# Attention's output product: eight fp32 blocks become split blocks with three fp32r products each

## What is computed

```python
def stick_breaking_attention(q, k, v):
    ...
        z = jnp.einsum('bhqd,bhkd->bhqk', q[:, :, q0:end], k[:, :, :end]).astype(jnp.float32) * scale
        ...
        log_stay = jnp.where(mask, -jax.nn.softplus(z), 0.0)
        stay_after = lax.cumsum(log_stay, axis=3, reverse=True) - log_stay
        log_w = jax.nn.log_sigmoid(z) + stay_after
        w = jnp.where(mask, jnp.exp(log_w), 0.0)
        o = jnp.einsum('bhqk,bhkd->bhqd', w, v[:, :, :end].astype(jnp.float32))

def stick_breaking_block(h, k, v, w_q, q_gain, w_o):
    q = rms_norm_2(heads(h @ w_q), q_gain)
    o = stick_breaking_attention(q, k, v)
    o = o.transpose(0, 2, 1, 3).reshape(Bt, S, D_ATTN)
    return o @ w_o

        x = x + stick_breaking_block(h, k_shared, v_shared, b_w_q[j], q_norm[j], b_w_o[j])
        x = x + 0.5 * swiglu(rms_norm_2(x, ffn2_norm[l]), ffn2_w13[l], ffn2_w2[l])
```

## Time and profile before

| | us |
|---|---|
| median of three executions | 1619.96 |
| the profiled execution | 1619.76 |
| its span, first to last instruction | 1618.0 |
| TensorE busy | 1571.3 (97%) |
| GpSimd busy | 917.8 (57%) |
| VectorE busy | 1035.1 (64%) |
| ScalarE busy | 737.9 (46%) |

### The profile page before, as it was taken

The page is one execution under the profiler, slowest core; times in us unless marked ns, Lnnn a source line. Parts: engine busy times, 40 slices in busy tenths (PEclk is TensorE's granted clock), DMA queues, the critical chain, the costliest instruction groups (busy, mean ns, idle before and its releaser), DMA issues.

```text
span 1618.0 us, 24581 instructions
## 1 busy us (share of the span) xinstructions
PE 1571.3 (97%) x9562; PEld 1361.0 (84%) x9562; DVE 1035.1 (64%) x1432; ACT 737.9 (46%) x1071; POOL 917.8 (57%) x1090
## 2 busy tenths in 40 slices
PE   7999999999999998999999999999999999899998
PEld 6888888877788887888888788888888888778887
DVE  6866565654686668966356686656676655468663
ACT  5554432022555454555333554555555553355452
POOL 6866520200796676966201796676977671179664
PEclk9999999999999999999999999999999999999999
DMA  7655532221465563655354465564465561146553
GB/s 269 208 185 184 180 118 93 79 73 51 164 208 183 182 202 122 211 193 168 134 180 145 157 215 181 177 221 144 151 216 185 171 215 40 66 157 214 185 173 117
DMA packets 107203, 263.65 MB, mean 163 GB/s; under 512 B 9168, under 2 KB 43088, under 8 KB 106960
## 3 DMA queue, kind: packets, MB, share of 16 engines
q1 hardware_dynamic: 107088, 262.09, 47.6%
HBM read 261.00 MB, written 1.05 MB: 162 GB/s over the span
## 4 chain that ended last, share of the span: by engine, by line
PE 90%; DVE 6%; ACT 1%; DMA 1%; issue 1%; POOL 1%; SPq 0%; DVEq 0%; ACTq 0%
PE ps L1597 39%; PE ps L1598 22%; PE ps L1645 9%; PE ps L1691 5%; PE ps L1600 4%; PE ps L1769 1%; DMA raw<-blocks 1%; DVE xn L903 1%; PE ps L1867 1%; DVE arena L1547 1%; PE ps L2066 1%; PE ps L1629 1%; PE ps L1630 1%; PE ps L1631 1%; PE ps L1661 1%
## 5 line engine op out<-in xcount | busy, mean ns | idle before, releaser
L517 POOL TENSOR_TENSOR w_lo<-raw,w_hi 128x256 fp32r<-128x256 f32 x1056 | 899.1, 885 | 582.9 <-ACT w_hi L595 579.3
L1597 PE MATMUL ps<-xn,w_hi 128*128 128x512 f32 x1848 | 664.4, 398 | 18.7 <-DVE xn L903 6.9
L1598 PE MATMUL ps<-xn,w_lo 128*128 128x256 f32 x2112 | 552.4, 281 | 0.0
L595 ACT ACTIVATE w_hi<-raw 128x1024 fp32r<-128x1024 f32 (+1 forms) x492 | 451.3, 927 | 211.3 <-PE ps L1600 114.4
L1597 PEld LDWEIGHTS ps<-xn,w_hi 128*128 128x128 f32 x1848 | 348.4, 189 | 98.2 <-DVE xn L903 10.0
L1598 PEld LDWEIGHTS ps<-xn,w_lo 128*128 128x128 f32 x2112 | 400.8, 190 | 17.3
L1597 PE MATMUL ps<-hid,w_hi 128*128 128x512 f32 x1008 | 363.6, 397 | 0.5 <-DVE w_lo L895 0.5
L1598 PE MATMUL ps<-hid,w_lo 128*128 128x256 f32 x1056 | 292.6, 282 | 0.0
L895 DVE TENSOR_TENSOR w_lo<-raw,w_hi 128x512 fp32r<-128x512 f32 (+1 forms) x222 | 253.0, 1140 | 33.1 <-ACT w_hi L595 28.1
L1597 PEld LDWEIGHTS ps<-hid,w_hi 128*128 128x128 f32 x1008 | 190.2, 189 | 41.9 <-issue 0.8
L982 DVE TENSOR_TENSOR arena<-ps,low_part 128x512 f32<-128x512 f32 x132 | 90.8, 688 | 200.4 <-ACT low_part L656 200.4
(11 more groups left out here) (320 smaller groups left out, 1243.6 us busy)
## 6 DMA issues: line engine op xcount, KB each, us to landing
raw<-blocks SPq DMA_DIRECT2D x419, 512.0 KB, 3.5
raw<-blocks SPq DMA_DIRECT2D x144, 256.0 KB, 3.5
cst<-consts SPq DMA_DIRECT2D x1, 2358.0 KB, 15.2
x<-x_in SPq DMA_DIRECT2D x4, 256.0 KB, 6.8
out<-x SPq DMA_DIRECT2D x4, 256.0 KB, 3.3
cst<-consts SPq DMA_DIRECT2D x1, 109.0 KB, 2.0
```

What stands on the lines that cost most here:

```text
L517: ins = nc.gpsimd.tensor_tensor(w_lo[:, slot(n), piece], raw[:, slot(n), piece], w_hi[:, slot(n), piece], ALU.subtract)
L595: nc.scalar.activation(w_hi[:, slot(n), cols], raw[:, slot(n), cols], ACT.Copy)\
L1597: nc.tensor.matmul(where, hi, both.rearrange("p a t -> p (a t)"), start=opens, stop=False)
L1598: ins = nc.tensor.matmul(where[:, 0:SEQ], lo, high, start=False, stop=False)
```

## The change

The eight blocks of w_o become split blocks (`split_out`), and the attention's outputs are split too: ScalarE writes the high half of pair c into `xn[:, c, 0, :]`, and VectorE subtracts it from the PSUM bank into `xn[:, c, 1, :]` (`y_low`). TensorE runs `output_rows` in place of `add_direct`: 24 fp32r matmuls for each block. Low parts of blocks 3, 5 and 7 are made on VectorE behind its loop, those of 0, 1, 2, 4 and 6 on GpSimd; before block 4 GpSimd waits until VectorE's eight products are done. ScalarE converts blocks 0 to 2 ahead of its first sigmoid. Ahead of the norm it now converts up to the third block of `ffn_f`, and the fourth and fifth stand inside the norm. Other phases' lists are unchanged.

```diff
-    add("attn_out", ["rows"] * 8)
+    add("attn_out", ["split_out"] * 8)
...
+def attn_out_on_vector(i):
+
+    return i in (3, 5, 7)
...
+                if phase == "attn_out":
+                    for i in range(KD):
+                        if i == 3:
+                            need(pool, "at_w", KD)
+                        if not attn_out_on_vector(i):
+                            lo(n0 + i)
...
+                    if a < len(late):
+                        hi_until(late[a])
                     nc.scalar.activation(squares(a, gains), pair_of_x(a), ACT.Square).then_inc(sq_ready, 1)
...
                 preload(ACT.Sigmoid)
+                hi_until(out_rows + 2)
                 need(act, "at_sep", 1)
...
                 def output(c):
                     need(act, "at_o", c + 1)
-                    nc.scalar.activation(y[:, c, :], bank(6 + c % 2)[:, 0, :], ACT.Copy).then_inc(ev["at_y"], 1)
+                    nc.scalar.activation(xn[:, c, 0, :], bank(6 + c % 2)[:, 0, :], ACT.Copy).then_inc(ev["y_hi"], 1)
...
-                hi_until(FIRST["attn_out"] + 8 + 4)
+                hi_until(out_rows + 8 + 2)
...
-                lambda: (norm(9, "g_ffn_f"), ffn(5, FIRST["ffn_f"]), hi_until(end)),
+                lambda: (norm(9, "g_ffn_f", late=(0, FIRST["ffn_f"] + 3, FIRST["ffn_f"] + 4)), ffn(5, FIRST["ffn_f"]), hi_until(end)),
...
+                def y_low(c):
+                    need(v, "y_hi", Y_BEFORE["attn_out"] + c + 1)
+                    signal(tt(xn[:, c, 1, :], bank(6 + c % 2)[:, 0, :], xn[:, c, 0, :], ALU.subtract), "y_lo")
...
                     if c == 1:
                         scaled_queries(3)
+                    if c >= 2:
+                        y_low(c - 2)
+                y_low(KD - 2)
+                lo(FIRST["attn_out"] + 3)
+                y_low(KD - 1)
+                lo(FIRST["attn_out"] + 5)
+                lo(FIRST["attn_out"] + 7)
...
+            def output_rows(phase, step, halves, low_weights):
+
+
+                n = FIRST[phase] + step
+                high, low = w_hi[:, slot(n), :], low_weights[:, slot(n), :]
+                need(pe, "y_hi", Y_BEFORE[phase] + step + 1)
+                pe.wait_ge(lo_ready[slot(n)], nth_split(n))
+                for which in (((0, 1, 2),) if step == KD - 1 else ((0, 1), (2,))):
+                    if 2 in which:
+                        need(pe, "y_lo", Y_BEFORE[phase] + step + 1)
+                    for d in range(KD):
+                        where, col = ps[:, d // 2, (d % 2) * SEQ:(d % 2 + 1) * SEQ], slice(d * P, d * P + P)
+                        for product in which:
+                            ins = nc.tensor.matmul(where, (high, low, high)[product][:, col], halves[:, product // 2, :],
+                                                   start=step == 0 and d % 2 == 0 and product == 0,
+                                                   stop=step == KD - 1 and d % 2 == 1 and product == 2)
+                        if step == KD - 1 and d % 2 == 1 and d < KD - 1:
+                            ins.then_inc(acc_done, 1)
+                ins.then_inc(used[slot(n)], 1)
...
-                        need(pe, "at_y", c - 1)
+                        need(pe, "y_lo", Y_BEFORE["attn_out"] + c - 1)
...
-                    need(pe, "at_y", i + 1)
-                    add_direct(FIRST["attn_out"] + i, y[:, i, :], start=i == 0, stop=i == KD - 1)
+                    output_rows("attn_out", i, xn[:, i, :, :], w_lo)
```

More of the change, by code:

```diff
@@ L121 @@
 LAST = dict(zip(ORDER, list(FIRST.values())[1:] + [NRING]))
+SPLIT_OUT = [phase for phase in ("mix_out", "lru_out", "attn_out") if KINDS[LAST[phase] - 1] == "split_out"]
+Y_BEFORE = {phase: KD * i for i, phase in enumerate(SPLIT_OUT)}
 UPDATES_BEFORE = {"ffn_a": 0, "ffn_b": 2, "ffn_c": 4, "ffn_d": 6, "ffn_e": 7, "ffn_f": 9}
@@ L194, in is_split @@
 def is_split(n):
-    return KINDS[n] in ("gate", "up", "near", "far", "far_short", "split_in", "split_rows")
+    return KINDS[n] not in ("in", "lru", "rows")
 def columns_of(n):
@@ L419, in build @@
             "proj_out gla_z gla_abs gla_ln gla_min gla_decay vt_done vt_out gla_qk sc_done sc_out o_done o_sq "
-            "on_done on_root y_ready y_gla y_hgrn y_pool y_rw lb_zero lb_exp fn_done pool_ready pool_done folds "
+            "on_done on_root y_ready y_hi y_lo y_gla y_hgrn y_pool y_rw lb_zero lb_exp fn_done pool_ready pool_done folds "
             "qk_made qk_done qk_out far_out "
@@ L455, in build @@
         weights_t = [carve(9490 + 768 * i, 6, P) for i in range(2)]
-        for name in ("lru_abs lru_ln lru_xc lru_gate_in lru_z lru_gelu lru_gates_done lru_ri lru_sp lru_a lru_m lru_root "
-                     "pad_rec heads_sq heads_n heads_root heads_ready q_sums q_root q_inv v_out at_z at_mask at_sig at_w at_wt "
-                     "at_wt_out at_o at_y at_sep col_done col_out").split():
+        for name in ("lru_abs lru_ln lru_xc lru_z lru_gelu lru_gates_done lru_ri lru_sp lru_a lru_m lru_root "
+                     "heads_sq heads_n heads_root heads_ready q_sums q_root q_inv v_out at_z at_mask at_sig at_w at_wt "
+                     "at_wt_out at_o at_sep col_done col_out").split():
             ev[name] = sem(name)
@@ L606, in preload, with norm @@
                 chain(nc.scalar.activation(table[:, 0:4], table[:, 4:8], func))
-            def norm(version, gains, then=ACT.Silu, after=None):
+            def norm(version, gains, then=ACT.Silu, after=None, late=(), behind=None):
                 for a in range(4):
@@ L630, in norm @@
                 preload(ACT.Sqrt)
+                if behind:
+                    hi_until(behind)
                 state["norms"] += 1
@@ L822, in attention @@
                 hi_until(FIRST["q_in"] + KD - 1)
+                out_rows = FIRST["attn_out"]
                 def token_roots(first, last):
```

## The result

The changed kernel takes 1623.97 us (median of 15 executions, 1621.81 to 1627.29), the kernel before 1619.35 (15 executions on the same chip). The ratio is 1.0023, with a 95% interval from 1.0016 to 1.0030: 3.7 us slower by the ratio, 4.6 by the medians. That is under the 0.3% bound of the prediction, and clearly not zero. The profiled execution of after took 1624.27 us, with a span of 1622.4.

What follows compares the result with a forecast made beforehand. VectorE's loop, after ScalarE's sigmoids, was taken to set the attention's pace, before TensorE's output matmuls. Terms: - 4.7 (output product) + 2.9 (conversions) + 2.3 (y_low) + 2.1 (GpSimd contention) - 0.2 (tail) = + 2.4, so 1622.3 us; range 1618.3 to 1626.0.

Steps and rivals of the forecast that it cites:

- the 0.3% bound of the prediction: Whole kernel time: about 0.3% (4.9 us) is what a measurement can tell from no change; chance of staying within it 0.76.

Runs made afterwards that it cites:

- e1: Changed kernel with the three w_hi conversions of output blocks 0 to 2 moved behind the first sigmoids and into the loop; 1622.35 us, 1.0014 of the kernel before.
- e2: Changed kernel with GpSimd's splits held until VectorE's eight products are done, from block 0 on instead of block 3; 1625.23 us, 1.0028 of the kernel before.
- e7: Kernel before with only ScalarE's new order (three feed-forward blocks ahead of the norm, two inside) and no split output blocks; 1622.48 us, 1.0016 of the kernel before.
- e8: Changed kernel without the eight y_low subtractions, the third product reading old low halves; 1622.60 us, 1.0015 of the kernel before.
- e3: Changed kernel with six unneeded fp32 matmuls on TensorE ahead of the matmuls that sum the squares; 1621.49 us, 1.0008 of the kernel before.
- e4: Changed kernel with ScalarE's old order restored: all five feed-forward conversions ahead of the norm; 1619.24 us, 0.9994 of the kernel before.
- e5: Changed kernel with the three w_hi conversions moved into the loop and ScalarE's old order ahead of the norm; 1616.79 us, 0.9984 of the kernel before.
- e6: Like e5, plus two unneeded fp32 matmuls on TensorE in each of attention turns 1 to 7; 1617.02 us, 0.9984 of the kernel before.
- e9: Changed kernel with GpSimd's low parts of the fourth and fifth feed-forward blocks held until VectorE's last sum; 1620.91 us, 1.0004 of the kernel before.

## What to carry to other kernels

When a change reorders one engine, ask what the moved work releases on the engines behind it: here two ScalarE conversions moved by a few microseconds put GpSimd beside the only VectorE operations that TensorE waits for, and cost 4.7 us. Price a wait of TensorE twice, by its length and by the clock it is followed by; a wait of 3.6 us that merely replaced lateness elsewhere cost 2.65 more. And when a change removes the cause of a wait, try it without the reorder that was meant to cure the wait: with the split blocks the old order was the better one, and with the conversions moved off the path the same change is 0.16% faster than before instead of 0.23% slower.

## What the runs showed of the hardware that I had not expected

- A fall of TensorE's clock came with each pause of about 3.5 us here (3.48 or 3.49 before the third logits, and 3.54 to 3.57 before the sum in after, e1, e2, e7 and e8), and none with the waits of 0.99 to 1.21 at the same place (before, e3, e4, e5, e6, e9). Behind the sum it added 1.8 to 2.9 to the time up to the end (187.4 to 188.5 against 185.6). The price varies because the low level began at different moments, between 2.0 us before the sum (e7) and the sum itself (e8). Over the 7 us from the sum on the granted clock was 0.56 (e2), 0.58 (after), 0.62 (e1), 0.65 (e7) and 0.76 (e8), and the times to the end fall in that order: 188.5, 188.4, 188.1, 187.9 and 187.4.
- Falls also came in the loop without such a pause, and not in the loop of before (1.00 throughout). Ahead of the one at 1392 in after TensorE was busy 3.80 of 7 us (1385 to 1392), and in the same stretch of before 3.92 of 7, with no fall behind it. What tells these apart was not settled; two unneeded products a turn (e6) removed them.
- An operation of VectorE with two inputs in SBUF waits for the rest of the GpSimd piece that is running, less 0.15 us. So a scan over 774 columns, 1.77 alone, takes 2.08 to 2.18, a product of 768 columns 1.25 to 1.32 instead of 0.96, and a sum of 512 columns 1.20 to 1.22 instead of 0.69: the loss doesn't grow with the operation. GpSimd's pieces of 0.72 take 1.44 beside a product and 2.19 beside a scan.
- The moment at which the attention begins varied by 4.8 us (1360.9 to 1365.6) between profiled executions with the same instructions ahead of it. At least part of it is the clock again: in the latest one (e8) it stood at 0.66 from 902 to 907 and at 0.62 from 1144.5 to 1149, where before has 1.00 from 895 to 910 and from 1137 to 1150. Two profiles must be compared from a common event, not from the start of the span.
